# Six modulation tiles placed beside the first projections, and the last two of the second layer ahead of the last residual sums

## The reference

```python
u = rmsnorm(h, norm_mix); proj = u @ w_in            # the first projections: q, k, then v
h = h + mixed @ w_out                                # the out-projection ("out1")
h = h + cross_attention(rmsnorm(h, norm_xattn), rmsnorm(mem, norm_mem), w_xq, w_xkv, w_xo)
h = h + experts(rmsnorm(h, norm_ffn))
x = rmsnorm(h, norm_final)
for l in range(2):
    mod = silu(c) @ w_mod[l] + b_mod[l]              # (1024) @ (1024, 6144), for c and for c_ctx
    sh1, sc1, ga1, sh2, sc2, ga2 = split(mod, 6)
    h = rmsnorm(x, g_norm1[l]) * (1 + sc1) + sh1
    x = x + ga1 * (mixer(h) @ w_out[l])
    h = rmsnorm(x, g_norm2[l]) * (1 + sc2) + sh2
    x = x + ga2 * (square(relu(h @ w_up[l])) @ w_down[l])
```

## Time and profile before

| | |
|---|---|
| median of 3 runs | 1630.34 us (1630.03 to 1632.29) |
| the profiled execution | 1625.92 us, of which the span of the engines' work is 1624.1 us |
| TensorE busy | 1559.8 us, 96% of the span |
| VectorE busy | 1060.2 us, 65% |
| ScalarE busy | 762.3 us, 47% |
| GpSimd busy | 99.5 us, 6% |
| DMA | 253.86 MB, mean 156 GB/s |

### The profile page before, as it was taken

One profiled execution on the slowest core, in us unless ns is written; L12 is line 12 of the kernel. 1 busy time (PEld: TensorE's weight loads), 2 busy tenths in 40 slices (PEclk: granted clock), 3 DMA queues, 4 the chain that ended last, 5 costly groups with the idle time before them and its releaser, 6 DMA issues.

```text
span 1624.1 us, 27286 instructions
## 1 busy us (share of the span) xinstructions
PE 1559.8 (96%) x9955; PEld 1370.4 (84%) x9955; DVE 1060.2 (65%) x1794; ACT 762.3 (47%) x1309; POOL 99.5 (6%) x165
## 2 busy tenths in 40 slices
PE   8999999999999999999899999999999998999997
PEld 7998788899999997875677888888887895899997
DVE  5577486788888879624755655555557846765564
ACT  5544544544444454444643641145224365665562
POOL 0011000000000000000300100010000001000000
PEclk9999999999999999999999999999999999999999
DMA  8666054487777733330331654455442452256552
GB/s 301 207 227 200 28 194 158 126 283 246 256 239 241 248 110 108 103 91 13 66 107 63 216 197 135 145 186 196 157 152 76 136 131 39 68 156 192 171 192 90
DMA packets 71497, 253.86 MB, mean 156 GB/s; under 512 B 7888, under 2 KB 11120, under 8 KB 71168
## 3 DMA queue, kind: packets, MB, share of 16 engines
q1 hardware_dynamic: 54048, 189.43, 35.3%
q0 software_dynamic: 17376, 63.44, 13.6%
HBM read 251.73 MB, written 1.11 MB: 156 GB/s over the span
## 4 chain that ended last, share of the span: by engine, by line
PE 84%; DVE 9%; ACT 3%; issue 3%; DMA 0%; DVEq 0%; SPq 0%; ACTq 0%
PE pair L1095 83%; ACT wh L585 1%; DVE uv L1775 1%; PE pair L1139 1%; DVE sq L2313 1%; DVE sq L1815 1%; DVE small L1807 1%; DVE wl L1734 1%; PE pair L1274 1%; ACT sq L653 0%; DVE spent L1867 0%; DVE uh_f L1867 0%; DVE ul L1764 0%; DVE res L2466 0%; DMA table<-in_table 0%
## 5 line engine op out<-in xcount | busy, mean ns | idle before, releaser
L1095 PE MATMUL pair<-uh,wh 128*128 128x256 f32 (+3 forms) x1864 | 581.8, 312 | 11.6 <-DVE ul L1764 5.5
L1734 DVE TENSOR_TENSOR wl<-ring,wh 128x1024 fp32r<-128x1024 f32 x350 | 427.1, 1224 | 248.3 <-ACT wh L585 242.2
L1095 PE MATMUL pair<-uh,wl 128*128 128x256 f32 (+3 forms) x1864 | 577.4, 310 | 0.0
L1095 PE MATMUL pair<-ul,wh 128*128 128x256 f32 (+3 forms) x1864 | 576.3, 309 | 0.0
L585 ACT ACTIVATE wh<-ring 128x1024 fp32r<-128x1024 f32 x350 | 367.4, 1052 | 260.6 <-PE pair L1095 253.4
L1095 PEld LDWEIGHTS pair<-uh,wh 128*128 128x128 f32 (+1 forms) x1864 | 346.6, 186 | 40.4 <-issue 13.4
L1095 PEld LDWEIGHTS pair<-ul,wh 128*128 128x128 f32 (+1 forms) x1864 | 346.3, 186 | 23.4
L1095 PEld LDWEIGHTS pair<-uh,wl 128*128 128x128 f32 (+1 forms) x1864 | 346.6, 186 | 23.0
L1095 PE MATMUL pair<-hh,wh 128*128 128x512 f32 (+1 forms) x512 | 172.9, 338 | 0.8
L1095 PE MATMUL pair<-hh,wl 128*128 128x512 f32 (+1 forms) x512 | 172.2, 336 | 0.0
L1095 PE MATMUL pair<-hl,wh 128*128 128x512 f32 (+1 forms) x512 | 172.2, 336 | 0.0
(11 more groups left out here) (279 smaller groups left out, 1983.8 us busy)
## 6 DMA issues: line engine op xcount, KB each, us to landing
ring<-in_w_stream SPq DMA_DIRECT2D x350, 512.0 KB, 3.8
uh_f<-in_mods POOLq DMA_DIRECT2D x48, 512.0 KB, 6.2
mod_w<-in_mods POOLq DMA_DIRECT2D x48, 512.0 KB, 3.8
uv<-c_rows POOLq DMA_DIRECT2D x4, 512.0 KB, 6.6
ml<-ml_dram POOLq DMA_DIRECT2D x4, 512.0 KB, 8.3
table<-in_table SPq DMA_DIRECT2D x1, 1849.5 KB, 12.0
res<-in_x SPq DMA_DIRECT2D x4, 256.0 KB, 4.1
res<-in_mem SPq DMA_DIRECT2D x1, 1024.0 KB, 14.3
```

The source lines that it names most:

```text
L1095: ins = pe.matmul(*operands, **flags)
L1734: tt(wl[:, s, :], ring[:, s, :], wh[:, s, :].bitcast(F32), ALU.subtract).then_inc(S("w_lo"), 1)
```

## The change

Six modulation tiles that stood in the output projections `out1` (four) and `xo` (two) are now computed in the first projections: three after the sixth, seventh and eighth step of the q/k projection, three between the steps of the v projection. The counts of the cross-attention's query projection stay at four, that of the first attention at eight; each place now works on other tile numbers. The six tiles have buffers of their own (`qk_w`, `qk_c`), in space that the cross-attention's keys and values use later, so ScalarE waits before it writes the first keys until they are used. GpSimd's list has two more loads of c, and its load of the context (`ctx_in`) stands behind the six tiles instead of at the front. In `add_to_res` the place of the (now empty) tile is between the two low parts of a step.

At the end of the first layer the loop of the last down-projection has three turns instead of four. The fourth is written out: two low parts, both modulation tiles, `mod_bias(1)`, the first residual sum, two low parts, the second residual sum, both sums of squares. TensorE's count on `spin` before the norm `n1_1` goes from 18 to 9.

```diff
-        "n2_0": (7, 17, 5), "n1_1": (18, 17, 6), "n2_1": (5, 8, 5)}
+        "n2_0": (7, 17, 5), "n1_1": (9, 17, 6), "n2_1": (5, 8, 5)}
...
+MOD_QK = 6
 MOD_FOX = range(0, 8)
-MOD_SB = range(0)
-MOD_OUT, MOD_XQ, MOD_XAT, MOD_XO = 4, 4, 0, 2
+MOD_OUT, MOD_XQ, MOD_XO = 0, 4, 0
...
+            load_c(qk_c)
+            for g in range(MOD_QK):
+                load_w(qk_w[g % 2], g, 0)
+            pool.wait_ge(S("u_v"), normed("mem")[1])
+            pool.dma_start(res[:, :, CTX], ctx_in).then_inc(S("ctx_in"), 16)
...
             for s in range(8):
                 split(S_QK + 2 * s + 1 + AHEAD)
...
                 if s == 4:
                     norm_tiles("mem", res, "g_mem", CTX, CTX)
+                if s >= 5:
+                    mod_tiles(1, spent[:, :, :])
...
+            for s in range(MOD_QK - 3):
+                mod_tiles(1, spent[:, :, :])
+                split(S_V + 2 + 2 * s + AHEAD - (s == 2))
             split(S_V + 5 + AHEAD)
             dve.wait_ge(S("fox_ln"), 1)
...
             def add_to_res(phase, name, first, mods):
                 for s in range(4):
+                    split(first + 2 * s + AHEAD - (s == 3))
+                    if s < mods:
+                        mod_tiles(1, spent[:, :, :])
                     split(first + 2 * s + 1 + AHEAD - (s == 3))
...
-                    if s < mods - 1:
-                        mod_tiles(1, spent[:, :, :])
                     if s >= 2:
                         add_square(name, s - 1, P, 512)
                 add_square(name, 3, P, 512)
                 split(first + 7 + AHEAD)
-                mod_tiles(1, spent[:, :, :])
...
-                    turns = 3 if ends else 4
+                    turns = 3 if nxt else 4
...
+                    elif nxt:
+                        lo_at[0] = pd + 12 + AHEAD
+                        split(pd + 16)
+                        late_two(3, 0)
+                        late_two(3, 1)
+                        late_two_keep(3)
+                        dve.wait_ge(S("macc_out"), MOE_TURNS + 2 + 16)
+                        mod_bias(1)
+                        for j in range(2):
+                            dve.wait_ge(S("job_full"), f0 + 6 + j)
+                            emptied(gated(0, 6 + j, bank[(b0 + j) % 4], 5), "dve")
+                            if j == 0:
+                                split(pd + 18)
```

More of the change, by code:

```diff
@@ L163 @@
 N_MOD = 48
+MOD_QK = 6
 MOD_FOX = range(0, 8)
-MOD_SB = range(0)
-MOD_OUT, MOD_XQ, MOD_XAT, MOD_XO = 4, 4, 0, 2
-MOD_MOE = len(MOD_FOX) + len(MOD_SB) + MOD_OUT + MOD_XQ + MOD_XAT + MOD_XO
+MOD_OUT, MOD_XQ, MOD_XO = 0, 4, 0
+MOD_MOE = MOD_QK + len(MOD_FOX) + MOD_OUT + MOD_XQ + MOD_XO
 assert MOD_MOE + N_UNIT - 2 == N_MOD
@@ L288, in build @@
         spent = at("spent", [P, 4, T], w0 + 12288)
+        qk_w = [at(f"qk_w{k}", [P, 4, T], w0 + 8192 + 1024 * k)[:, :, :] for k in range(2)]
+        qk_c = [at(f"qk_c{k}", [P, 4, T], w0 + 10240 + 1024 * k)[:, :, :] for k in range(2)]
         qx = at("qx", [P, KT, T], w0)
@@ L340, in mod_buffers @@
         def mod_buffers(g):
-            return (fox_w[g % 2], fox_c) if g < len(MOD_FOX) else (mod_w[0][g % 2], mod_c[0])
+            if g < MOD_QK:
+                return qk_w[g % 2], qk_c
+            return (fox_w[g % 2], fox_c) if g < MOD_QK + len(MOD_FOX) else (mod_w[0][g % 2], mod_c[0])
         def tab(name, rows=P):
@@ L480, in _ @@
             pool.memset(spin[:, :].bitcast(F32), 1.0).then_inc(S("spin_set"), 1)
-            pool.wait_ge(S("u_v"), normed("mem")[1])
-            pool.dma_start(res[:, :, CTX], ctx_in).then_inc(S("ctx_in"), 16)
             pool.wait_ge(S("c_silu"), 1)
@@ L515, in load_w @@
                 pool.dma_start(dst, src).then_inc(S(f"mod_in{g % 2}"), 16)
+            load_c(qk_c)
[3 more added lines that the diff above has]
+            pool.dma_start(res[:, :, CTX], ctx_in).then_inc(S("ctx_in"), 16)
             pool.wait_ge(S("job_full"), JOBS.full(JOBS.number("v", 3)))
             load_c(fox_c)
-            for g in range(len(MOD_FOX)):
+            for g in range(MOD_QK, MOD_QK + len(MOD_FOX)):
                 load_w(fox_w[g % 2], g, 0)
@@ L522, in _ @@
             load_c(mod_c[0])
-            for g in range(len(MOD_FOX), N_MOD):
+            for g in range(MOD_QK + len(MOD_FOX), N_MOD):
                 if g == MOD_MOE + 2:
@@ L707, in _ @@
                     b = full(act, "xkv", i)
+                    if i == 0:
+                        act.wait_ge(S("mod_used"), MOD_QK)
                     dst = kx[:, 2 * i:2 * i + 2, :] if i < 4 else vx[:, :, (i - 4) * T:(i - 3) * T]
@@ L1862, in mod_tiles @@
                         dve.wait_ge(S("mod_used"), g)
-                    if g in (0, len(MOD_FOX)):
-                        dve.wait_ge(S("mod_c_in"), 64 if g else 32)
+                    if g in (0, MOD_QK, MOD_QK + len(MOD_FOX)):
+                        dve.wait_ge(S("mod_c_in"), 32 if g == 0 else 64 if g == MOD_QK else 96)
                     w, c = mod_buffers(g)
@@ L1927, in _ @@
                     dve.tensor_copy(heads[r, 4 + g // 2, :], bank[7][r, 0:T]).then_inc(S("sb_out"), 1)
-                if h in MOD_SB:
-                    mod_tiles(1, pair[0][:, :].rearrange("p (a b) -> p a b", a=4))
                 if h == 6:
@@ L1968, in _ @@
                     divide(a + i)
-                if i == 1:
-                    mod_tiles(MOD_XAT, spent[:, :, :])
                 if 2 <= i < NX + 2:
@@ L2399, in late_one @@
                         if half == 0 and j == 0:
-                            dve.wait_ge(S("mod_c_in"), 96)
+                            dve.wait_ge(S("mod_c_in"), 128)
                         dve.wait_ge(S(f"mod_in{j % 2}"), i * 32 + 16 * (g // 2 + 1))
@@ L2485, in _ @@
                         down_turn(3, 3)
+                    elif nxt:
[11 more added lines that the diff above has]
+                                split(pd + 18)
+                        for j in range(2):
+                            dve.wait_ge(S("norm_sq"), SQ_AT[nxt] + 7 + j)
+                            dve.wait_ge(S("norm_add"), ADD_AT[nxt] + 6 + j)
+                            tt(sq[:, 3, 0:n], sq[:, 3, 0:n], sq[:, j, 0:n], ALU.add).then_inc(S("norm_add"), 1)
                     lo_at[0] = pd + MC + AHEAD
-                if l == 0:
-                    dve.wait_ge(S("macc_out"), MOE_TURNS + 2 + 16)
-                    mod_bias(1)
             dve.wait_ge(S("norm_rstd"), NORM["fin2"] + 1)
```

## The result

The changed kernel takes 1621.39 us in the median of 15 runs (1618.04 to 1627.65), the kernel before 1630.03 (1625.72 to 1634.68, 15 runs on the same chip). The ratio is 0.995, with a 95% interval of 0.9938 to 0.9962: 8.6 us faster by the medians, 6.2 to 10.1 by the interval. The forecast was 7.8 us.

What follows compares the result with a forecast made beforehand. TensorE bounds the kernel; VectorE's tiles cost time only where TensorE waits behind them. 3.8 + 1.4 + 2.6 - 0 = 7.8 us, so 1630.34 becomes 1622.5 us; likeliest case 1620.5 to 1624.5, eight in ten 1619 to 1626.5.

Steps and rivals of the forecast that it cites:

- The out-projection: Four tiles removed there: VectorE reaches the last residual sum on time, TensorE's matmul behind the norm comes 3.8 us earlier.
- The lower bound of 1.4: Out-projection: if the sum is late for another reason, only the tile ahead of the norm counts, 1.4 us.
- a sign of being wrong: Out-projection, profile after: a last residual sum more than 0.5 us behind the first `spin` would speak against the prediction.
- The projection xo: Two tiles removed there: only the one ahead of the norm costs time, 1.4 us; TensorE's wait falls from 2.34 to 0.9.
- The forecast place of the matmul, 295.1: TensorE's first matmul behind xo's norm, expected 5.2 us earlier than before, near 295.1.
- my sentence that the query projection sees the same loads at the same distances: Expert loop and query projection: the claim that their loads stay at the same distances; no time was charged for it.
- The end of the first layer: Both tiles move ahead of the sums, so the ones come at 1230.1 instead of 1232.69: 2.6 us, bounds 2.1 to 2.9.
- The first projections: Six tiles added there cost 0 us, hidden by VectorE's cover: 1.0 us at the tightest place, 2.5 at the end.
- one of my signs of being wrong: First projections, profile after: idle time of VectorE that ends by a load of `qk_w`.
- The sentence that even 6.2 us fits: First projections: tile loads, taken as 3.8 us, would be in time even at 6.2, being wanted 7.0 to 7.5 after issue.
- the first projections take something back: Rival, chance 0.12: 8 us loads or a late piece 15 cost TensorE up to 3 us there: 1623.5 to 1625.5.
- The rule on taking turns: DMA engines alternate between queues with work, so a tile's load beside a full ring would get half the rate.

Runs made afterwards that it cites:

- experiment 5: Changed kernel with three of the six tiles back behind the out-projection's residual sums, none ahead of its norm: 1624.89 us, ratio to before 0.9964.
- experiments 4 and 9: The changed kernel run again without edits, giving its second and third profiles: 1621.34 us (0.994 to before) and 1622.07 us (0.9949).
- experiment 7: Changed kernel with 18 instead of 9 matmuls on `spin` ahead of the second layer's first norm: 1625.05 us, ratio to before 0.9962.
- experiment 3: Changed kernel with loads and products of the six added tiles cut to 16 of 1024 elements: 1623.09 us, ratio to before 0.9945.
- experiment 6: Changed kernel with both products of each of the six added tiles made twice: 1635.08 us, ratio to before 1.0027.
- experiment 1: Kernel before with only the end of the first layer changed (fourth turn written out, 9 on `spin`): 1628.79 us, ratio to before 0.9985.
- experiments 8 and 10: Changed kernel with one query-projection tile moved into the out-projection and 4 instead of 9 `spin` matmuls behind the cross-attention's first scores: 1624.26 us (0.9958), again 1620.25 us (0.9948).

## Why the prediction was right

**The reading of the bound** held. Only waits of TensorE were worth anything: VectorE's busy time did not move (1060.2 and 1059.8 us) and the kernel became 8.6 us faster.

**The out-projection, 3.8 us: measured 3.7** (28.81 to 25.12), 3.8 in two other profiles. The mechanism was the forecast one (late sums), with the root, data, ending last afterwards. Counted from the restart in the first attention, the last sum was forecast at 18.9 us and came at 19.0, the end of the root at 23.2 and 23.3, TensorE's first matmul at 25.0 and 25.1. The lower bound of 1.4 for a case in which only the tile ahead of the norm counts was too high: experiment 5 has 0.2, since with the late sums the clock fell (0.57 from 220 to 224 us), and the slower ones hide the tile. The last sum came 0.81 us behind the first spin (216.11 and 215.30), more than the 0.5 that I had named as a sign of being wrong; it stood behind a low part that waited 1.05 us for ScalarE, whose high part stands in its list behind the square of the sum before. It cost next to nothing. In the third profile the sum came only 0.50 behind the first spin and TensorE waited 0.28 us for the squares instead of 0.60, yet the stretch took 25.13 us: the sum comes 19.0 us behind the restart in both, and it is the first spin that came earlier in the first one (18.22 us behind the restart against 18.54). The forecast had the spin at 18.7 and the sum 0.2 behind it. The spin came 0.5 early and the sum 0.1 late, so the sign tripped although the path held; why the spin comes at different times no row shows.

**The projection xo, 1.4 us: measured 1.4** in every profile with the change (wait of 2.34 to between 0.91 and 0.93). The forecast place of the matmul, 295.1, was missed by 2.0 us. Of those 1.8 are the late load of the tile ahead of the softmax, which my sentence that the query projection sees the same loads at the same distances passed over: a landing scatters, and that tile has little room for a late one (experiments 4 and 9).

**The end of the first layer, 2.6 us: measured 2.7** from first spin to ones, 2.8 to the matmul behind the norm. The gap before the ones was 0.50 us instead of 0.7. That eighteen matmuls would have come too late was right too (experiment 7).

**The first projections, 0 us: measured 0.0** (34.04 against 34.03, and 34.03 with the tiles cut in experiment 3), with a cover of 2.9 us instead of 2.5 (experiment 6). The step under it that failed is the load time: I took 3.8 us from `mod_w`, because the new buffers are plain rows, and it was 7.2, or 6.7 for the four loads in the stretch. A plain target does not make a load take 3.8 us: the same loads into the same buffers took 6.7 in the changed kernel and 3.8 in experiment 6, where VectorE's longer list spreads them out (issued some 7 us apart instead of 5). What differs is the traffic: the DMA engines are busy for 0.87 of the time from 60 to 80 us in the changed kernel and for 0.66 in experiment 6. Whether the form of the target has a part in the 6.2 us of `uh_f` stays open. The DMA issues from 50 to 85 us have, before and after,

```profile
ring<-in_w_stream SPq DMA_DIRECT2D x13, 512.0 KB, 4.3
```

```profile
ring<-in_w_stream SPq DMA_DIRECT2D x12, 512.0 KB, 6.2
qk_w<-in_mods POOLq DMA_DIRECT2D x4, 512.0 KB, 6.7
res<-in_ctx POOLq DMA_DIRECT2D x1, 1024.0 KB, 11.5
```

so the ring's loads take longer too with the tiles' beside them. The context's load, which took 6.1 us before, made ScalarE wait for a piece here, as forecast for its new place:

```profile
83.19 1.06 ACT L592 ACTIVATE wh<-ring 128x1024 fp32r<-128x1024 f32 x1 [3.31 <-DMA ring<-in_w_stream]
```

VectorE's low part behind it waited 0.33 us. For the loads of two tiles it waited 0.93 and 0.44 us, one of my signs of being wrong, and the instructions on `crow` began at 85.42 instead of 83.35 with TensorE untouched. The sentence that even 6.2 us fits was what carried the term. The rival *the first projections take something back* had this mechanism right, but not its size: it asked for 8 us from each of the four later loads, and the waits of 1.7 us in all stayed inside the cover. What was left of it is 1.2 us: VectorE was done with the last thing that the scores need (`spin`, written behind `crow`) at 88.62, and they started at 89.86. The term was right by that margin. The rule on taking turns stands in the Trainium skill's page "DMA: Bandwidth & Descriptors", section "Queues, rings and completion order". By my estimate from it a load beside a full ring gets half the rate; 6.7 against 3.8 us agrees with that, and no run tests the rule itself.

**The sum**, 7.8, lies in the interval of 6.2 to 10.1, and 1622.5 us is 1.1 from the median. That the whole fits as well as it does is in part luck: single runs of one kernel lie 9.6 us apart (1618.04 to 1627.65). The range of 1620.5 to 1624.5 does not follow from the bounds that I gave for the three gains: the lower ones (1.4, 1.4, 2.1) add up to 4.9 us, which is 1625.4. The places in the profile after were missed all the same (second layer 3.8 us earlier, not 7.8). From TensorE's wait for piece 13 (55.72 before, 55.82 after), after against before:

| up to | change so far, us | what came in between |
|---|---|---|
| experts (317.20 before) | -3.5 | two gains, and the late load |
| 798.18 | -2.7 | lower clock at 708 to 720 for longer than before's |
| 877.23 | -1.1 | lower clock at 796 to 800 |
| second layer (1238.72) | -3.9 | third gain |
| 1430.43 | -1.3 | lower clock at 1324 and at 1352 |
| last ones (1616.15) | +0.4 | slower pitch of matmuls, next section |

In the second profile of the changed kernel the same stations read -4.8, -3.6, -3.5, -6.2, -6.2 and -4.8.

## What to carry to other kernels

Look for the work that stands between a bound engine's last matmul and the chain that restarts it (sums, norm, root), and put it where the helping engine has a list of its own to hide in; write that list out with the times when each piece is needed, since the cover found so was right within 0.4 us here. Then shorten what was sized to fill the old wait. Take a load time from the stretch where the load will run, not from a buffer of the same shape elsewhere, and when the two profiles disagree with the medians, compare distances between rows that both have, stage by stage.

## What the hardware showed that I had not expected

**The clock falls in different places in executions of one kernel.** The stretch from 796 to 800 us, changed kernel, first and second profile (columns as in the earlier trace rows):

```profile
796.00:800.00 4.00, 4.00 (x22) 3.82 (x21) 2.81 (x7) 2.43 (x8) 3.82 (x7) 0.58 0.16 39
```

```profile
796.00:800.00 4.00, 4.00 (x31) 3.40 (x30) 3.02 (x8) 3.53 (x10) 3.82 (x8) 1.00 0.08 23
```

22 matmuls instead of 31. From TensorE's wait just before it (795.57 and 795.46) to the first matmul behind the next norm (876.22 and 874.64) the first profile took 80.65 us and the second 79.18, 1.5 us less. Over a profile the share of the clock not granted adds up to 6 us (second of the changed kernel, mean clock 0.996) to 18 us (experiment 1, mean clock 0.989). That is more than what any one term here is worth.

**TensorE's matmuls of 256 columns have two pitches at the full clock.** The second half of the last up-projection, before and after:

```profile
1536.00:1546.00 10.00, 10.00 (x91) 10.00 (x90) 6.16 (x8) 7.40 (x15) 0.00 (x0) 1.00 0.58 179
```

```profile
1536.00:1546.00 10.00, 10.00 (x87) 10.00 (x86) 6.18 (x7) 6.94 (x15) 0.00 (x0) 1.00 0.63 200
```

The loads and the code are alike, the engine is full, the clock is 1.00, and starts come every 0.113 or every 0.118 us. The stretch from 1523.66 to 1579.10 took 55.44 us before and 57.12 after. Over twelve profiles it is either 55.4 (four of them) or 57.1 (eight), with nothing in between; the two profiles of experiments 8 and 10 agree there, but differ by 1.3 us in the half before (45.81 and 44.55), so it is no property of a kernel. Experiment 1 met the slower pitch in the first projections too (34.87 instead of 34.03 us). What decides it stays open.
